# Loads, sums and a page layout in an NSA and Mamba-2 step: new order at the start, at two stage boundaries and in the sample attention

## The reference

```python
xp = xp + yp                                   # y: nsa_layer (i = 0) or ssd_layer (i = 1)
xs = xs + y_s
xp = xp + swiglu(rms_norm(xp, norm_ffn[i]), ffn_w_gate[i], ffn_w_up[i], ffn_w_down[i])
xs = xs + swiglu(rms_norm(xs, norm_ffn[i]), ffn_w_gate[i], ffn_w_up[i], ffn_w_down[i])
...
# nsa_layer: three branches per head, added with sigmoid gates
kc = rms_norm(compress_blocks(full_c[:, :, 0], cmp_pe[0], cmp_w1[0], cmp_w2[0]), qk_gain[1])
vc = compress_blocks(full_c[:, :, 1], cmp_pe[1], cmp_w1[1], cmp_w2[1])
o_c, o_s, o_w = nsa_attend(q, q_pos, kc, vc, full_s[:, :, 0], full_s[:, :, 1], win[:, :, 0], win[:, :, 1], w_pos)
o = gate[:, :, 0, :, None] * o_c + gate[:, :, 1, :, None] * o_s + gate[:, :, 2, :, None] * o_w
```

## Time and profile before

| | us |
|---|---|
| median of three runs | 2410.25 (2410.05 to 2411.53) |
| the profiled execution | 2412.8 |
| its span | 2411.1 |
| PE busy in it | 2226.6 (92%) |
| DVE busy | 1393.0 (58%) |
| POOL busy | 780.5 (32%) |
| ACT busy | 513.0 (21%) |
| mean granted clock of PE | 0.946 of full |

### The profile page before, as it was taken

One profiled execution on the slowest core, in us unless ns is written; L12 is line 12 of the kernel. 1 busy time (PEld: TensorE's weight loads), 2 busy tenths in 40 slices (PEclk: granted clock), 3 DMA queues, 4 the chain that ended last, 5 costly groups with the idle time before them and its releaser, 6 DMA issues.

```text
span 2411.1 us, 33614 instructions
## 1 busy us (share of the span) xinstructions
PE 2226.6 (92%) x11942; PEld 1756.9 (73%) x11942; DVE 1393.0 (58%) x2179; ACT 513.0 (21%) x1191; POOL 780.5 (32%) x661
## 2 busy tenths in 40 slices
PE   7998999998898579999989999998788999999899
PEld 6866877876565358888868787886454778888687
DVE  4447878655894135555742278785766355566522
ACT  1101112004675212111100132322542011111000
POOL 3311000003002743443333345552653344344242
PEclk9999999997999789999999999997988999999999
DMA  4134342404004952612111212220420202112112
GB/s 164 58 118 135 114 140 83 128 13 141 26 1 147 329 215 77 220 70 104 61 72 72 100 70 70 89 88 24 180 118 18 105 35 105 70 70 94 72 49 85
DMA packets 87447, 237.10 MB, mean 98 GB/s; under 512 B 11281, under 2 KB 60562, under 8 KB 72946
## 3 DMA queue, kind: packets, MB, share of 16 engines
q1 hardware_dynamic: 64130, 190.38, 22.0%
q0 software_dynamic: 7024, 29.90, 3.8%
q10 hardware_dynamic: 16128, 14.69, 1.9%
HBM read 218.46 MB, written 23.73 MB: 100 GB/s over the span
## 4 chain that ended last, share of the span: by engine, by line
PE 75%; DVE 14%; ACT 3%; issue 2%; SPq 2%; POOL 2%; DMA 1%; ACTq 1%; DVEq 0%; POOLq 0%
PE ps L341 55%; PE ps L944 6%; PE ps L466 1%; SPq L1733 1%; POOL sbuf L3029 1%; PE ps L1441 1%; PE ps L1454 1%; PE ps L1474 1%; DVE sbuf L2412 1%; ACT sbuf L1529 1%; PE ps L1324 1%; PE ps L858 1%; DMA sbuf<-win 1%; PE ps L2602 1%; SPq L1730 1%
## 5 line engine op out<-in xcount | busy, mean ns | idle before, releaser
L341 PE MATMUL ps<-sbuf 128*128 128x272 f32 x6048 | 1414.2, 396 | 47.1 <-DVE sbuf L2168 19.4
L341 PEld LDWEIGHTS ps<-sbuf 128*128 128x128 f32 x6048 | 1157.6, 192 | 300.9 <-issue 23.7
L391 POOL TENSOR_TENSOR sbuf<-sbuf 128x512 f32<-128x512 f32 (+2 forms) x90 | 136.3, 1514 | 769.5 <-PE ps L341 652.4
L360 ACT ACTIVATE sbuf<-ps 128x272 f32<-128x272 f32 x180 | 71.5, 397 | 1128.9 <-PE ps L341 1099.5
L944 PE MATMUL ps<-sbuf 128*128 128x256 f32 (+1 forms) x1280 | 301.0, 395 | 6.8 <-DVE sbuf L1087 6.8
L944 PEld LDWEIGHTS ps<-sbuf 128*128 128x128 f32 x1280 | 246.2, 194 | 59.9 <-issue 11.7
L371 DVE TENSOR_TENSOR sbuf<-sbuf,ps 128x272 f32<-128x272 f32 x90 | 39.4, 437 | 241.1 <-PE ps L341 240.1
L398 POOL TENSOR_TENSOR sbuf<-sbuf 128x512 f32<-128x512 f32 (+2 forms) x90 | 145.1, 1612 | 7.9 <-PE ps L341 1.2
L395 POOL TENSOR_TENSOR sbuf<-sbuf 128x512 f32<-128x512 f32 (+2 forms) x90 | 138.8, 1543 | 7.0
L392 POOL TENSOR_TENSOR sbuf<-sbuf 128x512 f32<-128x512 f32 (+2 forms) x90 | 137.4, 1526 | 7.1
L379 DVE TENSOR_TENSOR sbuf<-sbuf,ps 128x272 f32<-128x272 f32 x90 | 39.4, 438 | 128.2 <-PE ps L341 127.6
(11 more groups left out here) (360 smaller groups left out, 2350.2 us busy)
## 6 DMA issues: line engine op xcount, KB each, us to landing
sbuf<-w_gu SPq DMA_DIRECT2D x44, 1024.0 KB, 5.0
sbuf<-w_down SPq DMA_DIRECT2D x32, 704.0 KB, 5.4
sbuf<-w_ssd_in SPq DMA_DIRECT2D x20, 1024.0 KB, 4.8
sbuf<-cmp_pages SPq DMA_DIRECT2D x144, 128.0 KB, 2.4
sbuf<-cmp_pages ACTq DMA_DIRECT2D x112, 128.0 KB, 3.7
sbuf<-w_nsa_in SPq DMA_DIRECT2D x10, 1024.0 KB, 5.2
sbuf<-sel_k SPq DMA_DIRECT2D x64, 128.0 KB, 2.6
sbuf<-sel_v SPq DMA_DIRECT2D x64, 128.0 KB, 4.4
```

The lines of the kernel that those rows point to most:

```text
L341: last = pe.matmul(ps[:, bank_of(u, j), 0:HALF], a[:, kt * P:(kt + 1) * P], b[:, kt], start=kt == 0, stop=kt == kts - 1)
L360: do(act.activation(dst, bank_in(u, j), ACT.Copy), f_copied)
L391: do(pool.tensor_tensor(sv[:, 0], a21, a22, ALU.add), f_sums)
```

## The change

In eight places:

1. **Loads at the start.** The order becomes: the gains (36 columns of par), the first half of x, the first half of slot 0, the rest of x, the rest of slot 0, const_a, slot 1, the rest of par, slots 2 and 3. PE starts on the first half slot; DVE and ACT start on the gains and half of x; the remaining inputs are waited for where they are first read. POOL's third and fourth sum of unit 0 wait for DVE's four input sums.
2. **Entry of compression.** The row difference of T_MID for unit 0 is made by DVE in two halves, inside input units 8 and 9. The combined weight of T_MID is made by POOL, by four additions of 128x1024, behind its sums of unit 9.
3. **Rows of unit 1, part 1,** are issued by SP, not ACT.
4. **`second(0)`** is issued after T_LAST of unit 1, not after T_MID.
5. **Value pages** lie as eight partitions of 4096 floats (16 keys a row), page i on partitions 8i to 8i + 7. The turn of the selected branch reads every sixteenth column, so that the weights of a key meet its row.
6. **SP's order in the sample attention:** the key half of the next window goes ahead of the value unit. Loads are counted by place, not by unit.
7. **Feed-forward.** POOL's sums of v = 0 and of v = 22 wait for DVE's input sums. PE takes the sums of v = 22 one by one, and that unit frees its slots with the seventh product, not the fourth.
8. **Signals.** The gate's `g_neg` and `g_rows` and the store's `win_stored` go onto semaphores that are there already.

The diff, cut to its core:

```diff
@@ weight_sums
             do(pool.tensor_tensor(sv[:, 1], sv[:, 0], a11, ALU.subtract), f_sums)
+            if between:
+                between()
@@ p1_sp
-            sp.dma_start(xT, t["x"]).then_inc(x_in, 16)
-            sp.dma_start(par, t["par"]).then_inc(par_in, 16)
+            sp.dma_start(par[:, 0:GAINS], t["par"][:, 0:GAINS]).then_inc(x_in, 16)
+            sp.dma_start(xT[:, 0:KH], t["x"][:, 0:KH]).then_inc(x_in, 16)
+            sp.dma_start(ring[:, 0, 0:1024], t["w_nsa_in"][0][:, 0:1024]).then_inc(first_in, 16)
+            sp.dma_start(xT[:, KH:KT], t["x"][:, KH:KT]).then_inc(x_rest_in, 16)
+            sp.dma_start(ring[:, 0, 1024:SLOT], t["w_nsa_in"][0][:, 1024:SLOT]).then_inc(w_in[0], 16)
             sp.dma_start(ca, t["const_a"]).then_inc(ca_in, 16)
-            load_slots(sp, "nsa_in", t["w_nsa_in"], 4)
+            sp.dma_start(ring[:, 1], t["w_nsa_in"][1]).then_inc(w_in[1], 16)
+            sp.dma_start(par[:, GAINS:NPAR], t["par"][:, GAINS:NPAR]).then_inc(par_in, 16)
...
@@ p1_pe
                     if u == 0 and j == 2:
+                        pe.wait_ge(ca_in, 16)
                         norm1.pe(pe)
+                        in_slot(pe, s)
+                        pe.wait_ge(f_turns, TURNS_BEFORE["nsa_in"] + 3)
+                    if u == 0 and j == 5:
                         pe.wait_ge(f_turns, TURNS_BEFORE["nsa_in"] + 4)
@@ p1_dve, between the products' sums of units 8 and 9
+                    if (u, step) in FIRST_ROWS:
+                        part = FIRST_ROWS.index((u, step))
+                        dve.wait_ge(rows_in[0][part], 16 * NPAGE)
+                        first_rows(dve, do, part)
...
-                if u == 9:
-                    weigh(dve, do, 0, T_MID)
-                    transform(dve, do, 0, T_MID)
@@ p1_pool
+            raw_there(pool, 0)
+            pool.wait_ge(f_mm, multiplied(8, 6))
+            pool.wait_ge(in_ev, 18)
+            for a in (w_raw[0], w_of[T_MID]):
+                for h in (slice(0, 1024), slice(1024, SLOT)):
+                    pool_do(pool.tensor_tensor(w_of[T_MID][:, h], a[:, h], w_raw[1][:, h], ALU.add), c_mid)
@@ p2_sp
                 load_rows(sp, u, 0)
+                if u == 1:
+                    load_rows(sp, u, 1)
@@ p2_pe
-                    if j == T_MID and u >= 1 and u != PAIRS + 1:
+                    if j == (T_LAST if u == 1 else T_MID) and u >= 1 and u != PAIRS + 1:
                         second(pe, u - 1)
@@ p2_act
-                if u + 1 < NU:
+                if 1 <= u < NU - 1:
                     set_free(act, u + 1)
                     load_rows(act, u + 1, 1)
@@ first_rows (new)
+            d, at = rows_of(0), slice(part * NPAGE, (part + 1) * NPAGE)
+            do(dve.tensor_tensor(d[:, 3, at], d[:, 3, at], d[:, 1, at], ALU.subtract), c_t if part else None)
@@ p4_load_unit
+                if kind == "V":
+                    sp.dma_start(UNIT[place(kind, b)][i * rows:(i + 1) * rows],
+                                 src[bass.ds(page, 1)].rearrange("o (r j) n -> (o r) (j n)", r=rows)
+                                 ).then_inc(unit_in[place(kind, b)], 16)
+                    continue
@@ p4_sp
+                sp.wait_ge(sw_mm, pr + 1)
+                win_part(pr + 1, k_half, wk_in)
                 sp.wait_ge(ss_mm, pr + 1)
                 p4_load_unit(sp, "V", 2 * pr + 2)
-                sp.wait_ge(sw_mm, pr + 1)
-                win_part(pr + 1, k_half, wk_in)
@@ p4_pe, turn
-                        last = pe.transpose(ps[0:n, 6 + k % 2, (j - j0) * P:(j - j0 + 1) * P], S[:, j * P:j * P + n], ident)
+                        cols = S[:, j:PAST:NPAGE] if j < NPAGE else S[:, PAST:PAST + NS]
+                        last = pe.transpose(ps[0:n, 6 + k % 2, (j - j0) * P:(j - j0 + 1) * P], cols, ident)
@@ feed-forward, PE
+                        if v == GU_UNITS and j >= 3:
+                            pe.wait_ge(f_sums, 4 * u + {3: 2, 4: 2, 5: 3, 6: 4}[j])
                         elif j == 3:
                             pe.wait_ge(f_sums, 4 * u + 4)
                         first = product(pe, u, j, a, b, KH if gu else FH, before)
-                        if j == 3 and (v % 2 or not gu):
+                        if j == (6 if v == GU_UNITS else 3) and (v % 2 or not gu):
                             first.then_inc(w_used, 2 if gu else 4)
@@ feed-forward, POOL
+                    if v == 0:
+                        pool.wait_ge(f_turns, t0 + 4)
+                    if v == GU_UNITS:
+                        pool.wait_ge(f_turns, t0 + 4 + FH)
```

77 lines of the change are left out of this document (48 added, 29 removed).

## The result

The changed kernel takes 2461.84 us (median of 4 runs, 2455.15 to 2466.91) where the kernel before, on the same chip, takes 2410.89: a ratio of 1.0213, 95% interval 1.0198 to 1.0229. The forecast was 2375.5 us, with a range from 2364 to 2398. The profiled execution took 2455.15, its span is 2453.5.

A forecast was written before the change was run, and what follows sets the result against it. The prediction took TensorE (PE), three quarters of the last-ending chain, and what PE waits for to bound the kernel. Its terms −6.1 − 4.7 − 7.5 − 13.4 + 1.0 − 4.1 summed to −34.8: 2410.25 to 2375.5 us, range 2364 to 2398.

The forecast's parts named there:

- I take both at **zero: Sample attention: the new value page layout costs nothing, neither in the strided turn nor in the page load.
- rival C: Sample attention: value pages land slowly on 8 partitions, key pages queue behind; loss about 45 us, 2390 to 2421; chance 0.15.
- The bound that I had worked out: Value page load in sample attention: at worst 1/8 of the 418 GB/s, a unit in 40 us.
- the threshold of 24 us: Sample attention: a slow value unit costs time only from about 24 us a unit on.
- The sample attention without the layout: Window keys issued ahead of the value unit, two window-score waits go, POOL then sets the pace: −7.5 us.
- The start: Start of the kernel: reordered loads let PE begin at 8.1 instead of 14.35: −6.1 us.
- The entry of compression: PE's wait for DVE goes, 9.9 us freed at most, 5 turn into a wait at `second(1)`: −4.7 us.
- the chain that I named: Compression entry: unit 2's rows stay on ACT between `hide(0, 1)` and its next copies, delaying `second(1)`; unmoved, −3 us remains.
- The gate/down boundary: Feed-forward: gap at last gate/up unit goes, −12.0 us; later slot release adds 4.3 and 1.0: −6.7 a layer.
- The first units of the layers: Feed-forward: POOL's sums wait for DVE's turns; about +1.0 us in the first layer, −4.1 in the second.
- the sum of the forecast: Whole kernel: all terms added, −34.8 us, from 2410.25 to 2375.5.

The follow-up runs named there:

- vold: The changed kernel with the value pages as before (128 partitions of 256 floats a page), all else of the change kept: 2384.11 us, ratio 0.9878.
- vold_win: `vold` with SP's old order in the sample attention (value unit ahead of the next window's keys): 2384.52 us, 119.2 us in the stage.
- best_rows: Changed kernel, old value pages, sums product by product in all down units, no sums wait in feed-forward 0's first unit, compression unit 2's rows on SP: 2369.67 us.
- ffn_prod: `vold` with PE taking POOL's sums product by product and freeing slots with the seventh product in every down unit: 2375.38 us, ratio 0.984.
- combo: `ffn_prod` with ACT also copying the first products of compression unit 1 before it issues unit 2's rows: 2378.35 us, ratio 0.986.
- mix_sp: The changed kernel with the new value layout only for units that SP issues, POOL's pages as before: 2436.59 us.
- mix_pool: The changed kernel with the new value layout only for units that POOL issues, SP's value pages as before: 2439.63 us.

## Why the prediction was wrong

**The layout of the value pages** is the step that failed: "I take both at **zero**". For the turn that held, at 3.98 us a pair: every column of its weights starts a new line by the Trainium skill's rule on 16-byte lines ("SBUF — State Buffer", section "Door 1: The DMA port swizzle"), and against 3.86 to 3.97 before this cost nothing. For the load it did not hold: 71.8 us in place of zero. The reason that I gave under rival C was that "16 pages are under way at once and together cover all 128" partitions. They are issued together, but they reach half of the engines only, and where these keep step they write one page at a time, at 64 to 73 GB/s: at that rate 2 MB take 29 to 33 us. The bound that I had worked out (1/8 of the rate, 40 us a unit) was near, and the threshold of 24 us was passed; I chose the wrong end of a bound that I had right. In the changed kernel's own stage the packets of 16 KB took 0.98 us (POOL's) and 1.20 (SP's) on average, between the 2.02 of one page at a time and the 0.80 of the faster stretch, so 33 us is the worst case and not each unit's. The price of C was too low as well, 45 us: it counted a late value unit a pair. Behind it the whole queue of SP stood still, and 44.29 us of issue for one key unit were in no row of the kernel before. C's chance of 0.15, and 0.07 for slower, were far too small for a transfer of a shape that no row showed.

**The sample attention without the layout**: −7.5 forecast, −6.1 measured in `vold` against before, −7.6 against `vold_win`. The step held.

**The start**: −6.1 forecast, −5.3 in the changed kernel and −6.0 in `vold`. Rows that answer to the earlier trace rows; PE began at 8.58, the norm's 32 matmuls at 15.29:

```profile
8.58 6.88 PE L342 MATMUL ps<-sbuf 128*128 128x272 f32 x16 [8.58 <-DMA sbuf<-w_nsa_in]
...
15.29 7.54 PE L469 MATMUL ps<-sbuf 128*128 128x272 f32 x32
...
22.67 22.22 PE L342 MATMUL ps<-sbuf 128*128 128x272 f32 x96
```

**The entry of compression**: the mechanism was right, the size was not. In `vold` the first product of compression came 8.5 us earlier beyond the start's gain, since PE's wait of 6.82 us was gone; with the slow matmuls behind it the gain grew to 11.6. I expected half of 9.9 to be given back at `second(1)`, and −4.7 to stay. All but 1.3 us was given back in `vold` (−7.3, of which −6.0 came from the start). Over the eleven kernels with the same code so far, what stayed lies between −2.9 and +2.2 us (+2.2 in the changed kernel), so no execution reached −4.7. The term that was too small is what comes back at `second(1)`. Part of it is the chain that I named, unit 2's rows on ACT: without it `best_rows` keeps −6.2. I had counted the ACT issue, but not that the rows themselves land behind it, at 264. These rows of the changed kernel answer to the earlier trace rows:

```profile
233.66 2.29 DVE L1135 TENSOR_TENSOR sbuf<-sbuf 128x2048 f32<-128x2048 f32 x1 [8.45 <-DMA sbuf<-cmp_pages]
```
```profile
266.10 22.79 PE L986 MATMUL ps<-sbuf 128*128 128x256 f32 x96 [2.91 <-ACT sbuf L1064]
...
288.82 1.94 PE L882 MATMUL ps<-sbuf 128*64 128x512 f32 x8
```

**The gate/down boundary**: −12.0 a layer forecast, and −12.0 and −11.9 measured in `vold`. The new wait and the slow matmuls after it were 4.3 + 1.0 by my sum; together they took 4.8 us in the first layer and 5.0 in the second. So −7.2 and −6.9 for −6.7.

**The first units of the layers**: +1.0 forecast, +1.2 measured in the first (−9.6 to −8.4 in `vold`). In the second, −4.1 forecast: both waits for line 441 are gone and the norm takes 7.50 us again, but PE then waits 0.94 for the sums where I had put 0.2. The starts moved by 3.8 us, from −17.1 ahead of that unit to −21.0 behind it.

**Not forecast at all** was the prompt attention, which no part of the change touches. In `vold` it lost 4.4 us. Its matmuls were slower: the granted clock was 0.68 from 556 to 640 us, where the kernel before had 0.78 and `best_rows` 0.84 (before, `vold`, `best_rows`):

```profile
556.00:640.00 84.00, 68.58 (x522) 52.13 (x520) 57.88 (x221) 47.36 (x180) 19.49 (x37) 0.78 0.39 119
```
```profile
556.00:640.00 84.00, 73.36 (x511) 54.94 (x512) 54.79 (x218) 44.56 (x178) 19.00 (x36) 0.68 0.37 116
```
```profile
556.00:640.00 84.00, 67.24 (x528) 48.32 (x530) 63.20 (x246) 48.76 (x199) 18.39 (x35) 0.84 0.30 94
```

The stretch has short waits, and in stretches of 2 us the granted clock reads mostly 0.50 or 1.00, that is 1.2 or 2.4 GHz, at other moments in each kernel. Kernels that differ only later, as `vold` and `ffn_prod`, differ here too: prompt attention took 4.4 us longer in the one and 0.6 less in the other than before. Why is open; it was not tried. Single executions of one kernel lie more than 10 us apart (`combo` and `ffn_prod` have executions 13 and 12 us apart); each kernel has one trace, so that the clock is the reason is likely and not shown. Small gains were therefore read from the stage and not from the whole.

So without the page layout the sum of the forecast, −34.8, stood against −27.9 in `vold`. What was missing is 3.4 us at the entry of compression, 4.4 in the prompt attention, 1.4 in the sample attention and 0.7 in the rest of compression. Against that stand gains that I had not forecast: 1.4 at the output projection and 1.5 in Mamba-2, where no part of the change acts, and 0.7 at the two boundaries. So the 6.9 us by which the sum without the layout was off are what is left of about 10 us lost and 3.6 gained, and only part of either belongs to the change.

## What to carry to other kernels

A transfer has a shape at its destination, and a trace without that shape has no price for it. Before a tile is laid out for the engine that reads it, count the partitions, and how far apart they lie, that one transfer writes: pages of 128 KB on eight neighbouring partitions came in at 64 GB/s one at a time, and the same bytes, in as many issues, on 128 partitions held nothing up. Where such a load shares a queue, price not its own landing but that of all that is issued behind it. And when a wait is removed, ask for the second one right behind it: three of five places here gave back part of what they had gained. The same reading then removed the one at the boundary (4.8 and 5.0 us became 0.2 and 0.5) and part of the one in compression. Last, one trace is one execution: identical code reached the same matmul 5.8 us apart, so read a small gain from a near mark ahead of it, not from the start of the kernel.

## What the runs showed of the hardware

- Eight rows a transfer kept the DMA share at 0.48 to 0.55 and sixteen brought it to 1.04; the 0.5 holds for lone units of SP (`mix_sp`, 0.55) and of POOL (`mix_pool`, 0.51) alike.
- One page of eight rows at a time, the rate of a lone unit went by how far the rows lay apart: 64 and 73 GB/s (neighbours), 105 (sixteen apart), 209 (four apart). Sixteen rows gave 160 (neighbours) and 225 (eight apart).
- The same eight neighbouring rows came in at 166 GB/s in the changed kernel, where the packets did not start together: 0.80 us each in place of 2.02.
- A queue that is behind stops its issuer: SP's sixteen issues of key pages took 44.29 us.
- Loading weights by every sixteenth column cost TensorE nothing: 3.98 us for 17 transposes, against 3.86 to 3.97.
